# Keys in seven quarter products with a way through DRAM, modulation chunks and pooling averages under the values, the prompt's averages on VectorE

## The reference, cut to what matters

```python
h = _rmsnorm(x, g_norm1) * (1 + scale1) + shift1
proj = h @ w_in + b_in     # q, k, v, o, gates, u_pool, g_a, g_b
k = heads(k_raw) * (HEAD_DIM_M ** -0.5)
h_f, C_f, n_f, m_f = _mlstm_scan(q, k, v, i_f, log_sigmoid(f_f), ...)   # and backward
y_b = _pool_branch(u_pool, w_pool_grp, pool_scale, rows)
#   windows 2, 4, 8, 16: centred mean minus self; 1-D over the prompt, 2-D over the 8 x 64 latent grid
merged = sigmoid(g_a) * (y_a @ w_proj_a) + sigmoid(g_b) * (y_b @ w_proj_b)
x = x + gate1 * (merged @ w_out)
```

## Time and profile before

| | us |
|---|---|
| median of 3 runs | 962.71 (962.21 to 964.01) |
| the profiled execution | 961.65 |
| its span | 959.8 |
| TensorE busy in the span | 935.3 (97%) |
| VectorE busy | 706.0 (74%) |
| ScalarE busy | 489.0 (51%) |
| GpSimd busy | 136.0 (14%) |

### The profile page before, as it was taken

How to read it: one execution, slowest core, us unless ns; L and a number is a source line. 1 busy time by engine, 2 the same in 40 slices (tenths; PEclk the granted TensorE clock), 3 DMA queues, 4 the chain that set the end, 5 groups by cost and what they waited for, 6 DMA issues and landing times.

```text
span 959.8 us, 14248 instructions
## 1 busy us (share of the span) xinstructions
PE 935.3 (97%) x5618; PEld 829.0 (86%) x5618; DVE 706.0 (74%) x922; ACT 489.0 (51%) x651; POOL 136.0 (14%) x141
## 2 busy tenths in 40 slices
PE   7999999999999999999999999989999999999986
PEld 5799999978788999999999988868888888888862
DVE  5798777559223488989454546369999999999998
ACT  5565442131312456666311232247787887887763
POOL 0000000199910101001000000020112111111100
PEclk9999999999999999999999999979999999999999
DMA  9814442288671343335382155159999999999964
GB/s 371 343 44 134 150 131 103 80 305 313 236 298 73 99 144 100 94 122 200 109 328 88 45 209 208 45 204 408 421 419 405 424 420 414 414 416 413 395 275 162
DMA packets 39634, 229.39 MB, mean 239 GB/s; under 512 B 4336, under 2 KB 4784, under 8 KB 19088
## 3 DMA queue, kind: packets, MB, share of 16 engines
q1 hardware_dynamic: 26928, 180.12, 47.8%
q0 software_dynamic: 10048, 41.70, 12.2%
q10 hardware_dynamic: 2592, 6.66, 1.8%
HBM read 205.81 MB, written 22.66 MB: 238 GB/s over the span
## 4 chain that ended last, share of the span: by engine, by line
PE 91%; DMA 4%; DVE 3%; issue 1%; SPq 0%; ACT 0%; DVEq 0%; POOLq 0%; ACTq 0%
PE ps L1984 85%; PE ps L2042 2%; DMA raw<-in_wst 1%; PE ps L2516 1%; DMA h2scr<-ht 1%; PE ps L2544 1%; PE ps L2031 1%; PE ps L2358 0%; DMA xg<-h2scr,slot_rows 0%; PE ps L2259 0%; DVE rowA L1939 0%; DVE xr L1942 0%; DVE xr L1946 0%; PE ps L2435 0%; DMA rowB<-yscr 0%
## 5 line engine op out<-in xcount | busy, mean ns | idle before, releaser
L706 ACT ACTIVATE whi<-raw 128x2048 fp32r<-128x2048 f32 x18 | 34.4, 1911 | 95.9 <-PE ps L1984 63.4
L1984 PE MATMUL ps<-hhi,whi 128*128 128x320 f32 x352 | 81.2, 312 | 0.0
L1984 PE MATMUL ps<-hhi,wlo 128*128 128x320 f32 x352 | 80.2, 309 | 0.0
L1984 PE MATMUL ps<-hlo,whi 128*128 128x320 f32 x352 | 78.9, 309 | 0.0
L1795 DVE TENSOR_TENSOR olo<-raw,ohi 128x2048 fp32r<-128x2048 f32 x32 | 72.4, 2289 | 3.9 <-ACT ohi L1073 3.9
L1795 DVE TENSOR_TENSOR wlo<-raw,whi 128x2048 fp32r<-128x2048 f32 x31 | 70.3, 2290 | 5.3 <-ACT whi L1073 4.7
L1169 DVE TENSOR_TENSOR wlo<-raw,whi 128x2048 fp32r<-128x2048 f32 x18 | 41.9, 2327 | 40.4 <-ACT whi L706 40.4
L1073 ACT ACTIVATE whi<-raw 128x2048 fp32r<-128x2048 f32 x32 | 61.3, 1918 | 18.9 <-PE ps L1984 18.9
L1073 ACT ACTIVATE ohi<-raw 128x2048 fp32r<-128x2048 f32 x32 | 61.3, 1918 | 18.0 <-PE ps L1984 18.0
L1984 PEld LDWEIGHTS ps<-hhi,whi 128*128 128x128 f32 x352 | 58.6, 188 | 6.2 <-issue 4.2
L1984 PEld LDWEIGHTS ps<-hhi,wlo 128*128 128x128 f32 x352 | 58.8, 188 | 0.0
(11 more groups left out here) (429 smaller groups left out, 2574.8 us busy)
## 6 DMA issues: line engine op xcount, KB each, us to landing
raw<-in_wexp SPq DMA_DIRECT2D x64, 1024.0 KB, 9.2
raw<-in_wst SPq DMA_DIRECT2D x59, 1024.0 KB, 6.2
eraw<-in_wexp SPq DMA_DIRECT2D x32, 1024.0 KB, 8.6
nm<-negscr POOLq DMA_DIRECT2D x8, 640.0 KB, 7.0
wib<-wiscr POOLq DMA_DIRECT2D x8, 512.0 KB, 6.1
thscr<-gout ACTq DMA_DIRECT2D x12, 320.0 KB, 4.8
TH<-thscr POOLq DMA_DIRECT2D x3, 1280.0 KB, 7.8
xT<-in_x SPq DMA_DIRECT2D x4, 640.0 KB, 6.0
```

The costliest lines, as they stand in the source:

```text
L706: act.activation(dst[:, :], raw[raw_slot(c)][:, :], ACT.Copy).then_inc(hi_ready, 1)
L1984: return nc.tensor.matmul(out, lhsT, rhs, start=start, stop=stop)
```

## The change

Three things move together.

The keys become four more pairs in seven products, between the gate pairs and the query pairs (`SPILLS` = 10, `PAIRS` = 14). As the place of the keys is covered by the input sums, `finish_block` scales and biases each key block in place and `spill` writes it to `thscr`. GpSimd reads them back (`keys_back`): head 0 at once, heads 1 to 5 after the pooling, heads 6 and 7 later. `score` waits for them.

The sixteen modulation chunks, which lay between the key blocks, lie between the value blocks (`MOD2_AFTER`), as do their turns; the stream order of the chunks keeps the pattern, with value chunks where the key chunks were.

The pooling on GpSimd still starts at the end of the pairs. Its latent part stays on GpSimd, with buffers in the place of keys 1 to 5. The prompt's part goes to VectorE (`prompt_window`), with its own counts `rcnt_c`. The calls stand behind the gate scans, and the semaphore `s_cp` counts them; GpSimd waits for it before it loads the counts of the next window size. `score(0, .)` now waits for the end of the pooling (`D_U`).

```diff
-N_U, N_GE, N_Q, N_K, N_MOD2, N_V, N_O, N_GL, N_B, N_A, N_OUT = 2, 6, 4, 4, 16, 4, 4, 2, 2, 4, 4
-PAIRS = N_GE + N_Q
+N_U, N_GE, N_K, N_Q, N_MOD2, N_V, N_O, N_GL, N_B, N_A, N_OUT = 2, 6, 4, 4, 16, 4, 4, 2, 2, 4, 4
+SPILLS = N_GE + N_K
+PAIRS = SPILLS + N_Q
 AT_U0, AT_M1, AT_U1 = 0, 1, N_MOD1 + 1
 AT_GE = AT_U1 + 1
-AT_K = AT_GE + PAIRS
-AT_V = AT_K + N_K + N_MOD2
-AT_O = AT_V + N_V
+AT_V = AT_GE + PAIRS
+V_AT = (0, 3, 8, 13)
+AT_O = AT_V + N_V + N_MOD2
 AT_GL = AT_O + N_O
 AT_B = AT_GL + N_GL
...
-        vb = at("vb", 178.5, [P, D])
-        mst = at("mst", 183, [P, 4, 2, KT])
-        mrows = at("mrows", 184, [64, P])
+        vb = at("vb", 148, [P, D])
+        mst = at("mst", 4.75, [P, 4, 2, KT])
+        mrows = at("mrows", 5, [64, P])
...
-        XP = [at(f"XP{i}", 152 + 2.5 * i, [P, GR, GW + 2 * PAD]) for i in range(2)]
-        RP = [at(f"RP{i}", 157 + 3.75 * i, [P, 2 * GR - 1, GW]) for i in range(2)]
-        CP = [at(f"CP{i}", 164.5 + 0.625 * i, [P, TC + 2 * PAD]) for i in range(2)]
-        rcnt = at("rcnt", 166, [P, T])
+        XP = [at(f"XP{i}", 134.5 + 2.5 * i, [P, GR, GW + 2 * PAD]) for i in range(2)]
+        RP = [at(f"RP{i}", 139.5 + 3.75 * i, [P, 2 * GR - 1, GW]) for i in range(2)]
+        CP = [at(f"CP{i}", 174.75 + 0.5625 * i, [P, TC + 2 * PAD]) for i in range(2)]
+        rcnt_c, rcnt_l = at("rcnt_c", 175.875, [P, TC]), at("rcnt_l", 202.75, [P, TL])
...
+        D_RCNT = [16 + 32 * (g + 1) for g in range(NG)]
+        D_U = D_RCNT[-1] + 16
+        D_KEYS = D_U + 16, D_U + 32
+        D_U2, D_ZERO = D_U + 48, D_U + 64
...
-                if c == AT_V + 1:
+                if c == m2_chunk(4):
                     sp.wait_ge(d_const, 16)
-                    sp.wait_ge(d_pool, 16 * (NG + 1))
+                    sp.wait_ge(g_mm, PRODUCTS * PAIRS)
+                    sp.wait_ge(g_cmb, PRODUCTS * PAIRS)
...
+            gp.wait_ge(g_cmb, PRODUCTS * PAIRS)
             gp.memset(gOne[:, :], 1.0).then_inc(s_init, 1)
+            for b in range(2):
+                gp.wait_ge(d_tile[b], SPILLED)
+
+            def keys_back(a, b):
+                gp.dma_start(QK[:, H + a:H + b, :], thscr[2 * N_GE + a:2 * N_GE + b, :, :].rearrange(
+                    "f p t -> p f t")).then_inc(d_pool, 16)
+
+            keys_back(0, 1)
             for g, w in enumerate(WIN):
                 gp.wait_ge(u_out, g + 1)
-                gp.dma_start(rcnt[:, :], rcnt_d[:, g, :]).then_inc(d_pool, 16)
+                if g:
+                    gp.wait_ge(s_cp, g)
+                gp.dma_start(rcnt_c[:, :], rcnt_d[:, g, 0:TC]).then_inc(d_pool, 16)
+                gp.dma_start(rcnt_l[:, :], rcnt_d[:, g, TC:T]).then_inc(d_pool, 16)
                 st.on(gp.memset(XP[0][:, :, :], 0.0))
-                st.on(gp.memset(RP[0][:, :, :], 0.0))
-                st.do(gp.memset(CP[0][:, :], 0.0))
...
-            gp.sem_inc(s_pool, 1)
+            gp.wait_ge(s_cp, NG)
             gp.dma_start(uscr, U[:, :, :]).then_inc(d_pool, 16)
-            gp.memset(Vt[:, :, :, DH:V1], 1.0).then_inc(s_init, 1)
+            gp.wait_ge(d_pool, D_U)
+            keys_back(1, H - 2)
             gp.wait_ge(d_rows, 32)
             gp.wait_ge(s_modT, KT + 2)
             chunk_used(gp, m2_chunk(N_MOD2 - 1))
...
+            gp.wait_ge(d_pool, D_KEYS[0])
+            keys_back(H - 2, H)
...
-            def gate_tanh(j, b):
+            def finish_block(j, b):
                 act.wait_ge(g_cmb, PRODUCTS * j + 7 - b)
                 out, f = gout[b][:, :], 2 * j + b
-                act.activation(out, out, ACT.Tanh, scale=0.5, bias=col[:, 36 + f:37 + f])\
-                   .then_inc(g_ev, 1)
+                if j < N_GE:
+                    ins = act.activation(out, out, ACT.Tanh, scale=0.5, bias=col[:, 36 + f:37 + f])
+                else:
+                    f += H - 2 * N_GE
+                    ins = act.activation(out, out, ACT.Identity, scale=SCALE, bias=col[:, f:f + 1])
+                ins.then_inc(g_ev, 1)
 
             def spill(j, b):
...
+            act.wait_ge(g_mm, PRODUCTS * PAIRS)
+            split_hi(v_at(1), QH[1])
+            log_sigmoid()
+            act.wait_ge(v_ready, NT)
+            split_hi(v_at(2), QH[0])
+            mod_row2(0)
...
+            def prompt_window(g):
+                w = WIN[g]
+                dve.wait_ge(u_out, g + 1)
+                if g:
+                    dve.wait_ge(s_cp, g)
+                st.do(dve.memset(CP[0][:, :], 0.0))
+                st.do(dve.tensor_copy(CP[0][:, PAD:PAD + TC], U[:, g, 0:TC]))
+                n, s, src = TC + 2 * PAD, 1, 0
+                while s < w:
+                    n -= s
+                    st.do(dve.tensor_tensor(CP[1 - src][:, 0:n], CP[src][:, 0:n],
+                                            CP[src][:, s:s + n], ALU.add))
+                    s, src = 2 * s, 1 - src
+                cs = CP[src][:, PAD - w // 2:PAD - w // 2 + TC]
+                dve.wait_ge(d_pool, D_RCNT[g])
+                st.do(dve.tensor_tensor(CP[1 - src][:, 0:TC], cs, rcnt_c[:, :], ALU.mult))
+                dve.tensor_tensor(U[:, g, 0:TC], CP[1 - src][:, 0:TC], U[:, g, 0:TC],
+                                  ALU.subtract).then_inc(s_cp, 1)
...
+            prompt_window(0)
+            split_lo(v_at(2), QH[0], QL[0])
+            prompt_window(1)
+            mod_add(0)
             dve.wait_ge(d_const, 32)
             dve.wait_ge(s_init, 2)
-
+            for t in range(NT):
+                value_rows(0, t)
+            split_lo(v_at(3), QH[1], QL[1])
+            prompt_window(2)
+            prompt_window(3)
...
+            mod_add(1)
+            mod_rows()
             dve.wait_ge(s_gt, 3)
             dve.wait_ge(d_late, 32)
             mask_maxima(0)
...
                 value_rows(1, t)
...
+            MOD2_AFTER = {(0, 0): 0, (0, 2): 2, (0, 4): 4, (1, 1): 6, (1, 3): 8, (2, 0): 10, (2, 2): 12,
+                          (2, 4): 14}
             for c in range(N_V):
                 for t in range(NT):
                     value_block(c, t)
-                    if c == 0 and t == 2:
+                    at = MOD2_AFTER.get((c, t))
+                    if at is not None:
+                        mod2_product(at)
+                        mod2_product(at + 1)
+                    if (c, t) == (1, 2):
+                        mod2_turned(0)
+                    if (c, t) == (2, 3):
+                        gate_rows()
+                    if (c, t) == (3, 1):
                         mod2_turned(1)
-                    if c == 0 and t == 4:
...
+                if i == 0 and h in (1, H - 2):
+                    pe.wait_ge(d_pool, D_KEYS[h > 1])
...
-            pe.wait_ge(q_free, 3 + 2 * N_K)
+            pe.wait_ge(g_cmb, PRODUCTS * PAIRS)
+            pe.wait_ge(d_pool, D_U)
```

More of the change, by code:

```diff
@@ L397, in layer_kernel @@
         d_nm, d_wib = [sem(f"d_nm{s}") for s in range(2)], sem("d_wib")
[L398 to L399 removed]
+        m_done, v_ready, v_free, o_ready, o_free = (
+            sem(n) for n in ("m_done",
                              "v_ready", "v_free", "o_ready", "o_free"))
@@ L404, in layer_kernel @@
         s_o, s_hd, s_yh, s_yl = (sem(n) for n in ("s_o", "s_hd", "s_yh", "s_yl"))
-        s_pool, s_ybh, s_mg, s_mgh, s_mgl, s_mst = (sem(n) for n in (
-            "s_pool", "s_ybh", "s_mg", "s_mgh", "s_mgl", "s_mst"))
+        s_cp, s_ybh, s_mg, s_mgh, s_mgl, s_mst = (sem(n) for n in (
+            "s_cp", "s_ybh", "s_mg", "s_mgh", "s_mgl", "s_mst"))
         t_mm, t_ev, t_xr, t_sq, t_rs, t_h2, t_tp, t_ht, t_lg = (sem(n) for n in (
@@ L921, in _ @@
             act.wait_ge(v_ready, 3 * NT)
-            act.wait_ge(d_ms, 16)
             act.wait_ge(d_rows, 32)
+            act.wait_ge(d_pool, D_U)
             for d in range(2):
@@ L1528, in head_rows @@
                                          ALU.mult, ALU.add).then_inc(pv_free, 1)
-            split_lo(AT_V + 2, QH[0], QL[0])
-            for t in range(NT):
-                value_rows(0, t)
-            split_lo(AT_V + 3, QH[1], QL[1])
-            dve.wait_ge(raw_free[raw_slot(AT_V + 3)], raw_use(AT_V + 3) + 2)
+            chunk_used(dve, AT_O - 1)
             def gate_lo(f):
@@ L1553, in _ @@
             scale_queries(0)
+            dve.wait_ge(d_pool, D_U)
             chunk_states(0)
@@ L2175, in _ @@
                 product(j, 6, 6, *b22)
-            def block_k(j, b):
-                e = 2 * j + b
-                if b == 0:
-                    chunk_split(k_at(j))
-                pe.wait_ge(q_free, e + 1)
-                for k in range(KT):
-                    o = (b * KT + k) * P
-                    last = three([(ps[:, KEY_BANK[e % 3] + a, 0:HALF], cut_half(a)) for a in range(2)],
-                                 QH[j % 2][:, o:o + P], QL[j % 2][:, o:o + P], hhi[:, k, :], hlo[:, k, :],
-                                 k == 0, k == KT - 1)
-                last.then_inc(q_ready, 1)
             def mod2_turned(g):
-                pe.wait_ge(m_done, g)
+                if g:
```

(12 more changed lines are left out.)

171 lines of the change are left out of this document (56 added, 115 removed).

## The result

The changed kernel takes 979.61 us (median of four runs, 977.65 to 979.74) against 962.46 us of the kernel before on the same chip: a ratio of 1.0171, with a 95% interval of 1.0153 to 1.0188. It is slower; the medians lie 17.2 us apart. The prediction said 984.0.

What follows compares the result with a forecast made beforehand. TensorE bounds the kernel; 48 fewer matmuls save 7.0 us, but the later pooling chain delays the first output-gate product by 19.2 us, plus 2 for clock restart: profiled 982.9, median 984.0 us, range 972 to 994.

Steps and rivals of the forecast that it cites:

- The signs that the prediction named: Next profile: fourteen pairs of 12.3 us, scans of 512 at 1.25, GpSimd idle about 20, TensorE idle well over 10.
- Rival 1: Before the scores: pooling, maxima and value rows all hidden within E + 74, so faster, 955.7 us; chance 0.05.
- Rival 2: In the values: only TensorE's 7.2 us wait for modulation chunk 9 counts, about 965 us; chance 0.05.
- Rival 3: VectorE against GpSimd: every VectorE instruction delays GpSimd (+3.5 us), scans stay at 29 us (+11.8), or one: 988 to 999; chance 0.10.
- E: The end of the last pair, from which the steps count: 188.06 us before, predicted at 237.3 after.
- Step 1: After the pairs: VectorE reaches the gate scans at E + 15.8 instead of E + 19.9.
- Step 2: Scans on VectorE: 17.5 us (bounds 17 and 29), first prompt window 1.3; `s_cp` rises at E + 34.7.
- Step 3: GpSimd's windows 4, 8 and 16: 49.7 us including 8 of VectorE's contention, ending at E + 84.4; bounds 44 and 54.
- Step 4: Behind the windows: copy 4.9 us, maxima 7.0, masking and value rows; scores at E + 99.6, first output-gate product E + 102.3.
- Step 5: TensorE before the scores: idle from about E + 82, a hidden stall on chunk 9, and 2 us for the clock.
- the restart: TensorE's start after idling before the scores: 2 us lost to the half-level clock; bounds 0 and 5.

Runs made afterwards that it cites:

- paced kernel: The change with GpSimd's latent averages under the pairs, one window size per two pairs, halted midway; prompt's averages on VectorE behind first-half value rows: 967.43 us, ratio 1.0055.
- bare one: The change with all running averages left out, head 0's maxima in the other buffer, own prompt counts and VectorE's masking later: 958.38 us, ratio 0.9959.
- own counts: The change with a separate prompt-count buffer for each window size, so GpSimd no longer waits for VectorE's prompt window: 983.60 us, ratio 1.0218.
- without averages: The change without the pooling's running averages on GpSimd and VectorE, third value chunk's split between the two pairs of scans: 961.34 us, ratio 0.9989.
- split first: The paced kernel with VectorE splitting the fourth value chunk before the prompt's four windows instead of behind them: 959.88 us, ratio 0.9974 to the kernel before.
- filler products: The change with 85 unread matmuls of 320 columns on TensorE in its idle time before the scores: 978.87 us, ratio 1.0156.

## Why the prediction was right, step by step

**The mechanism.** It is the forecast's own: 48 products fewer, and a chain that starts at the end of the pairs, sleeps until VectorE is through with the scans, and ends 13.75 us after TensorE is ready for it. The signs that the prediction named are all there: fourteen pairs of 12.3 us, scans of 512 at 1.2 us, GpSimd idle for 17.84 us until VectorE, and `nmd`, `nm` and GpSimd behind TensorE's idle time. Rival 1 (all hidden) fell by the 13.75 us of idle time. Rival 2 (only the chunk's stall) fell by the same idle time, and the run that removes the stall is not faster (982.29 us). Rival 3 (more contention) fell: the scans ran alone in 15.4 us. The key pairs cost nothing by themselves. How near the number came is in part luck: the scans and the windows were put 6.3 us too long together, the maxima and the clock 3.1 us too short.

**The pairs.** E was predicted at 237.3; the first value product is at 237.41.

**Step 1** put the scans at E + 15.8; they start at 252.25, E + 14.8.

**Step 2** put `s_cp` at E + 34.7. It is at 269.0, E + 31.6. The scans are 15.41 us and not 17.5 (below the lower bound of 17 too). The reductions that the step lists, 3.4, 3 and 5 us off 29.3, give 17.9 and not the 17.5 written. The passes over 640 columns had been lengthened by 4.5 us where I took off 3; the first four scans (3.7) and the short steps (5.4) were nearer. The prompt window is 1.35 us, as said (1.3).

**Step 3** gave the three windows 49.7 us; from 269.01 to their last subtraction's end at 315.50 they took 46.5, inside the bounds of 44 and 54. What I had wrong is who waits. I charged GpSimd with VectorE's contention. In the changed kernel's rows it is mostly VectorE that waits for GpSimd; GpSimd loses some 4 us where I charged 8 (2.0 in a copy, 2.0 in the last size's four adds, 7.12 us against 5.17 with the prompt's averages on GpSimd). VectorE first and GpSimd below:

```profile
276.40 2.47 DVE L1444 TENSOR_TENSOR Vt<-ps,vb 128x512 f32<-128x512 f32 x4
...
287.58 3.92 DVE L1432 TENSOR_TENSOR CP<-CP 128x143 f32<-128x143 f32 x3
```

```profile
276.30 2.89 POOL L578 TENSOR_TENSOR RP<-RP 128x640 f32<-128x640 f32 x2
...
284.87 2.59 POOL L556 COPY XP<-U 128x512 f32<-128x512 f32 x1
```

Three adds of the prompt take 3.92 us beside GpSimd's, where one takes 0.31 us alone. GpSimd's copy of 0.61 us takes 2.59 us beside a split of 2.29 us. The value rows, with one operand in PSUM, take their usual 0.62 us each beside GpSimd's adds, and the adds theirs. This is the rule of the Trainium skill (SBUF — State Buffer, "SBUF: two separate sides") on which the step leaned: an exclusive lock for a whole instruction, taken where VectorE reads two operands from SBUF or runs in a two-port mode. The trace agrees, in both directions; the prompt's copies, with one operand, were held up as well (1.47 us at 294.73 against 0.23 alone), which falls under the second condition if such a copy runs in that mode, and no run here shows whether it does.

**Step 4.** The copy was there 5.5 us after the windows, and 5.2 were said. The maxima took 8.3 us and not 7.0, above the upper bound of 8. The first QK product was predicted at 336.9 and is at 332.44, 4.5 us earlier: steps 1 and 2 gave 3.1, step 3 gave 3.2, and step 4 took back 1.8.

**Step 5.** The stall on chunk 9 was 4.0 us, not 7.2, and hidden as said. For the clock I took 2 us at the restart. The granted clock was 0.50 from 321.9 on, 3 us into the idle time, and through the first scores, and the score stage took 3.26 us against 2.09 before: 1.2 us. The Trainium skill (TensorE: Matmul & The Clock Gate, "What's actually happening") has the half level after an idle stretch; the row of 330 to 334 now shows it. But the spans differ by 18.1 us and the marks at 335.70 by only 15.3. Matched one by one, VectorE's and ScalarE's instructions lie 15.2 us later than before up to the router, 16.5 behind it, and 18.2 in the end of the last stage. The two steps lie where the changed kernel has two more stretches at the half level, far from the change:

```profile
655.80:659.20 3.40, 3.40 (x12) 2.42 (x11) 2.46 (x3) 0.00 (x0) 3.21 (x3) 0.59 0.47 146
...
950.00:953.50 3.50, 3.50 (x5) 1.35 (x4) 3.08 (x3) 0.01 (x1) 0.00 (x0) 0.52 1.02 411
```

The kernel before has the same code there at 640 and 932, at 1.00:

```profile
639.00:644.00 5.00, 3.02 (x18) 2.47 (x19) 3.61 (x3) 0.00 (x0) 4.26 (x3) 1.00 0.34 105
...
932.00:937.00 5.00, 3.85 (x9) 1.82 (x10) 4.64 (x6) 1.50 (x2) 0.00 (x0) 1.00 1.02 407
```

So the clock cost about 4.0 us where I had 2: 1.2 at the restart, inside the bounds, and 2.8 at places that I had no term for (by their place; no run takes these two stretches away alone). I forecast 21.2 us between the two profiled executions and there are 18.1: 4.5 less by the chain, 1.4 more by the clock and the score stage together. The remaining 1.2 us of the 4.4 by which the median was missed is the distance between median and profiled execution, which I took over from before (1.06) and which is -0.13 after.

## What to carry to other kernels

A wait that protects nothing but a buffer can still set a good order: taking GpSimd's wait away alone didn't make the kernel faster (a ratio of 1.0218 against 1.0171), since the scans that it then ran beside doubled, and TensorE hung on what VectorE had queued behind them. When a stage is shortened, list every chain that starts at its beginning and is due at its end, the loads too: here the maxima and the initial states both stood behind the averages, and with the maxima issued earlier TensorE waited for the states. Work moved under a full stage isn't free because its engine has room: with GpSimd busy for 93 of 99 us the pairs lost 6.6 us, and with 64 of 94 us, halted in between, 0.4. The second kernel also leaves the prompt's averages to VectorE; how much of the gain is the pacing and how much the smaller work wasn't separated.

## What the runs showed of the hardware

The same copy to `uscr`, 1280 KB, kept GpSimd waiting for 4.6 us in the change and 5.4 in the paced kernel, 5.9 in the bare one and 6.8 with the prompt's averages on GpSimd, and for 10.7 to 11.5 us in the kernels with own counts, without averages and with the split first. The DMA share from its issue to its landing doesn't put them in order: 0.64 in the change, 0.83 in the paced kernel and 1.06 in the bare one, against 1.00, 0.87 and 0.82 in those three. I had taken a load's time as fixed; what sets it stays open.

Stretches of 3.4 to 10.2 us at the half level turn up in the router and in the last stage, and which piece of the work they meet shifts with everything ahead of them. In the run without averages the scores are 3.6 us early and the end is 0.3 us late; with filler products 2.2 us behind the router were given back in the last stage. What sets the place of such a stretch stays open. A gain of 2 to 3 us at one place of this kernel can be gone at its end for this reason alone.
